# Gates of the second block as three products of split parts, with the mixers' buffers moved

## What is computed

```python
h = rmsnorm(x, norm1_g[l])
z = h @ w_in[l]
z_mla, z_nsa, z_fox, z_dsa, z_gate = split_cols(z, [MLA_COLS, NSA_COLS, FOX_COLS, DSA_COLS, GATE_COLS])
o_mla, o_nsa, o_fox, o_dsa = four attention mixers of 4 heads of 64
branches = jnp.stack([o_mla, o_nsa, o_fox, o_dsa], axis=2)
lifted = jnp.einsum('bsnc,ncd->bsnd', branches, w_branch[l])
gates = jax.nn.sigmoid(z_gate.reshape(B, S, 4, 1024))
mixed = jnp.sum(gates * lifted, axis=2)
x = x + mixed @ w_out[l]
h2 = rmsnorm(x, norm2_g[l])
x = x + jnp.square(jax.nn.relu(h2 @ w_up[l])) @ w_down[l]
```

## Time and profile before

| | us |
|---|---|
| median of three runs | 1879.98 |
| profiled execution | 1882.94 |
| its span, first to last instruction | 1881.2 |
| TensorE busy | 1702.9 (91%) |
| VectorE busy | 874.6 (46%) |
| ScalarE busy | 728.1 (39%) |
| GpSimd busy | 557.7 (30%) |
| mean granted TensorE clock | 0.950 of full |

### The profile page before, as it was taken

How to read it: one execution, slowest core, us unless ns; L and a number is a source line. 1 busy time by engine, 2 the same in 40 slices (tenths; PEclk the granted TensorE clock), 3 DMA queues, 4 the chain that set the end, 5 groups by cost and what they waited for, 6 DMA issues and landing times.

```text
span 1881.2 us, 21970 instructions
## 1 busy us (share of the span) xinstructions
PE 1702.9 (91%) x8908; PEld 1385.5 (74%) x8908; DVE 874.6 (46%) x1587; ACT 728.1 (39%) x1030; POOL 557.7 (30%) x190
## 2 busy tenths in 40 slices
PE   6999989989787799897999977999999999879997
PEld 1844767776586677777888765999888887659996
DVE  1865567765364887535233254222351432542321
ACT  2423367543232676334222343444441123444442
POOL 0400015524211155325200016564531000355554
PEclk9999789999888899998989999999999999989999
DMA  9367169955360589642342415455533433145551
GB/s 386 133 231 267 56 248 343 341 210 195 109 243 15 205 331 342 239 135 88 110 149 90 157 47 177 136 191 188 170 118 113 148 117 114 61 157 178 192 182 43
DMA packets 46645, 327.17 MB, mean 174 GB/s; under 512 B 5456, under 2 KB 5456, under 8 KB 8784
## 3 DMA queue, kind: packets, MB, share of 16 engines
q1 hardware_dynamic: 46544, 325.76, 48.5%
HBM read 324.69 MB, written 1.05 MB: 173 GB/s over the span
## 4 chain that ended last, share of the span: by engine, by line
PE 72%; DVE 18%; ACT 4%; DMA 2%; issue 1%; POOL 1%; SPq 0%; DVEq 0%; ACTq 0%; POOLq 0%
PE ps L201 27%; PE ps L204 14%; PE ps L205 14%; PE ps L206 14%; DVE lo L212 6%; DVE acc L220 2%; ACT hi L209 2%; DMA raw<-in_wmod 1%; DVE hTl L212 1%; DVE xn L212 1%; DVE gl L212 1%; PE ps L2556 1%; DMA raw<-in_wgu 1%; DVE ar L212 1%; DVE x L212 1%
## 5 line engine op out<-in xcount | busy, mean ns | idle before, releaser
L212 POOL TENSOR_TENSOR lo<-raw,hi 128x2048 fp32r<-128x2048 f32 (+2 forms) x100 | 466.3, 4674 | 717.5 <-ACT hi L209 717.5
L209 ACT ACTIVATE hi<-raw 128x2048 fp32r<-128x2048 f32 (+2 forms) x216 | 396.2, 1864 | 70.4 <-DMA raw<-in_wo_hx 28.6
L212 DVE TENSOR_TENSOR lo<-raw,hi 128x2048 fp32r<-128x2048 f32 (+1 forms) x116 | 324.5, 2814 | 125.2 <-ACT hi L209 125.2
L201 PE MATMUL ps<-hT,raw 128*128 128x256 f32 x1024 | 234.5, 386 | 0.0
L201 PEld LDWEIGHTS ps<-hT,raw 128*128 128x128 f32 x1024 | 193.7, 192 | 30.4 <-issue 3.6
L204 PE MATMUL ps<-hTh,hi 128*128 128x256 f32 x640 | 183.7, 287 | 4.6 <-POOL hTl L212 4.6
L205 PE MATMUL ps<-hTl,hi 128*128 128x256 f32 x640 | 183.0, 286 | 0.0
L206 PE MATMUL ps<-hTh,lo 128*128 128x256 f32 x640 | 182.9, 286 | 0.0
L204 PE MATMUL ps<-hi,gh 128*128 128x512 f32 x320 | 133.1, 416 | 14.4 <-DVE lo L212 14.4
L204 PE MATMUL ps<-hi,hTh 128*128 128x512 f32 (+3 forms) x320 | 118.7, 371 | 17.9 <-DVE hTl L212 10.5
L212 POOL TENSOR_TENSOR big<-big 128x512 f32<-128x512 f32 x16 | 20.3, 1269 | 376.9 <-DVE big L220 376.9
(11 more groups left out here) (285 smaller groups left out, 2836.7 us busy)
## 6 DMA issues: line engine op xcount, KB each, us to landing
raw<-in_wgu SPq DMA_DIRECT2D x64, 1024.0 KB, 5.3
raw<-in_wmod SPq DMA_DIRECT2D x48, 1024.0 KB, 5.3
raw<-in_wdn SPq DMA_DIRECT2D x32, 1024.0 KB, 4.9
raw<-in_wgt SPq DMA_DIRECT2D x32, 1024.0 KB, 4.8
raw<-in_wup SPq DMA_DIRECT2D x32, 1024.0 KB, 4.8
raw<-in_wdown SPq DMA_DIRECT2D x32, 1024.0 KB, 5.1
raw<-in_wz SPq DMA_DIRECT2D x12, 1024.0 KB, 4.8
raw<-in_wbr SPq DMA_DIRECT2D x8, 1024.0 KB, 6.9
```

The costliest lines, as they stand in the source:

```text
L201: return self.e.matmul(o, l, r, start=first, stop=last)
L209: return self.e.activation(o, a, f, **kw)
L212: return self.e.tensor_tensor(o, a, b, op)
```

## The change

The gates' chunks become split chunks ("dve"): ScalarE writes the high part, VectorE the low part over the raw chunk, and a gate is eight `mm3` with `hTh` and `hTl` in place of eight float32 matmuls with `hT`. `a_fill` and `v_fill` split gt0 and gt1 before the first gate, and after every second gate (after g1 gt2, after g3 gt3, and so on to gt15 after g27) the chunk two further. While the mixers run, the high parts have a ring of two buffers: the one left before, and the memory of `hT`, which the gates no longer read (free from the new key "z done"). The raw ring has four slots (RMIX) in place of five. The fifth holds the transposed probabilities `pT` and the compressed windows' small tiles (`up`). The probabilities `pbs` move from `ar` to the memory of `oh` and `ohT` (`pb`). The chunks of compress (cmp, two) are asked for just before their products, behind gt0 and gt1 in the queue where they were behind gt0 alone. The chunk of latent (mla) is asked for behind gt12.

```diff
-NR, RFREE, NH = 7, 5, 5
+NR, RFREE, RMIX, NH = 7, 5, 4, 5
@@ class Book
-        self.before = dict(R=[None] * NR, H=[None] * NH)
+        self.before = dict(R=[None] * NR, H=[None] * (NH + 1))
...
-    def enter(self):
+    def enter(self, free, *key):
 
         self.epoch += 1
-        self.rings["R"] = [r for r in self.rings["R"] if r < RFREE]
+        if key:
+            self.rings["H"], self.before["H"][NH] = [NH - 1, NH], key
+        self.rings["R"] = [r for r in self.rings["R"] if r < free]
 
     def leave(self, *key):
 
         self.epoch += 1
-        self.rings["R"] += range(RFREE, NR)
+        back = [r for r in range(NR) if r not in self.rings["R"]]
+        self.rings["R"] += back
         self.rings["H"] = [NH - 1, *range(NH - 1)]
-        self.before["R"][RFREE:] = [key] * (NR - RFREE)
-        self.before["H"][:-1] = [key] * (NH - 1)
+        for r in back:
+            self.before["R"][r] = key
+        self.before["H"][:NH - 1] = [key] * (NH - 1)
...
     if name == "gt":
-        return t_in["wgt"][at[0], at[1], at[2]], "raw"
+        return t_in["wgt"][at[0], at[1], at[2]], "dve"
@@ class Tiles
-        self.hi = [at(f"hi{i}", a, PIECE, dt=F32R) for i, a in enumerate(hs)]
+        self.hi = [at(f"hi{i}", a, PIECE, dt=F32R) for i, a in enumerate([*hs, self.hTat])]
...
+        self.up, self.pb = at("up", rs[RMIX], 2048), at("pb", ohat, 2048)
@@ views2
-        V.pbs = [ar[:, 4096:5120], ar[:, 5120:6144]]
+        V.pbs = [pb[:, 0:1024], pb[:, 1024:2048]]
...
-                 for p in (ar[:, 6144:7680], gr[:, 0:1536])]
-        V.cmpb = ar[:, 7680:8080]
+                 for p in (up[:, 0:1536], gr[:, 0:1536])]
+        V.cmpb = up[:, 1536:1936]
@@ t_fill
                 if n % 2 == 0:
                     c = t.chunk("gt", l, d, n // 2)
-                    wv = kn(c.raw, 8)
+                    wh, wl = kn(c.hi, 8), kn(c.lo, 8)
                 b = t.take("B", "gate", l, d, n)
-                t.wait_ge(*t.at("landed", c.key))
+                t.wait_ge(*t.at("lo", c.key))
                 t.wait_ge(*t.free(b))
                 for k in range(8):
-                    m = t.mm(self.ps[:, b, 0:256], wv[:, k, 128 * (n % 2):128 * (n % 2) + 128], self.hT[:, k, :],
-                             k == 0, k == 7)
+                    m = t.mm3(self.ps[:, b, 0:256], [q[:, k, 128 * (n % 2):128 * (n % 2) + 128] for q in (wh, wl)],
+                              [q[:, k, :] for q in self.H3], k == 0, k == 7)
@@ a_fill
         a.wait_ge(*a.at("used", ("z", l, 5, 1)))
+        self.a_split(a, "gt", l, 0, 0, ahead=1)
         for d in range(8):
             for n in range(4):
...
                 a.ac(V.sg[:, n, d, :], self.ps[:, b, 0:256], ACT.Tanh, scale=0.5).then_inc(*a.up(f"free{b}"))
+                if n % 2:
+                    self.a_split(a, "gt", l, d, n // 2, ahead=2)
                 yield
@@ v_fill
+        self.v_split(v, "gt", l, 0, 0, ahead=1)
         for d in range(8):
             for n in range(4):
+                if n % 2:
+                    self.v_split(v, "gt", l, d, n // 2, ahead=2)
                 yield
@@ t_compress
-        w2 = [t.chunk("cmp", l, s) for s in range(2)]
...
         for s in range(2):
-            wcv = w2[s].raw.rearrange("p (m d) -> p m d", m=32)
-            t.wait_ge(*t.at("landed", w2[s].key))
+            c = t.chunk("cmp", l, s)
+            wcv = c.raw.rearrange("p (m d) -> p m d", m=32)
+            t.wait_ge(*t.at("landed", c.key))
@@ t_latent
-        wm = t.chunk("mla", l)
         yield
...
         yield
+        wm = t.chunk("mla", l)
         t.wait_ge(*t.at("landed", wm.key))
@@ tensor, first block
-        t.book.enter()
+        t.book.enter(RFREE)
@@ tensor, second block
             self.t_z(t, l)
-            t.book.enter()
+            t.mark("z done", l)
+            t.book.enter(RMIX, "z done", l)
             self.t_mixers(t, l)
```

More of the change, by code:

```diff
@@ L368, in __init__ @@
         self.z = sb("z", 2, 2520)
+        ohat = self.where
         self.oh, self.ohT = sb("oh", 2, 640, dt=F32R), sb("ohT", 5, 256, dt=F32R)
@@ L1988, in views2 @@
     def views2(self):
-        ar, big = self.ar, self.big
+        ar, up, pb, big = self.ar, self.up, self.pb, self.big
         A = lambda a, n, i: ar[:, a:a + n].rearrange("p (i n) -> p i n", i=i)
@@ L2389, in t_compress @@
             m.then_inc(*t.up(f"full{b}" if s else "pe"))
-            t.mark("used", w2[s].key)
+            t.mark("used", c.key)
         yield
```

## The result

The changed kernel takes 1903.19 us (median of four, 1902.27 to 1906.17) beside 1879.98: the ratio is 1.012, with a 95% interval of 1.0095 to 1.0144. The forecast had the sign right (slower) and less than half of the size: +9.5 us against +23. The profiled execution took 1902.27 us with a span of 1900.5, where that of before had 1882.94 and 1881.2.

A forecast was written before the change was run, and what follows sets the result against it. TensorE was taken as the bound, with almost no idle time in the gates. Per layer, 21.4 us of waits less 17.6 saved, plus 1.2 for the clock, gave +10 us over two layers: 1889.5 us, range 1864 to 1905.

The forecast's parts named there:

- The saving: Gates on TensorE: 2.88 us each in place of 3.43, saving 17.6 us a layer if nothing waits.
- The moves at no cost: Moved buffers and chunks cost nothing; if the cover for the last chunks is gone, up to 3 us a layer.
- Place 1: Start of the gates: 4.9 us idle before g0, then 2.1 behind index rotations and key copies; together 7.0.
- Place 2: Compressed windows: chunk gt2 lands late and its high part delays the window copies; 2.5 us idle.
- Place 3: Compressed probabilities: VectorE reaches them late, between low parts 6 and 7; 1.0 us, an estimate of 0 to 2.
- Place 4: First softmaxes: low parts among top-k passes, then exps and chunk 10's split delay g20; 2.7 us idle.
- Place 5: Latent: 1.5 us idle behind nwin maxima and latent norms, then 2.8 before g22; together 4.3.
- Place 6: Banks: 2.1 us idle inside the latent transposes and 1.8 before g28; together 3.9.
- The clock: TensorE's granted clock falls once a layer after idle time: +1.2 us a layer, 0 to 4 possible.
- the fall at every wait: Rival: the clock falls at all six places, 1.5 us each; +3.8 + 9 a layer, 1905 us, chance 0.12.
- the cover holds: Rival: only places 1 and 2 stay, 9.5 of 17.6 us; -8 a layer, 1864 us, chance 0.24.
- Half of them: Rival: places 3 to 6 cost 7 to 9 us in place of 11.9; within 3.8 us of 1880, chance 0.16.

The follow-up runs named there:

- the products alone: Changed kernel with three float32r products a step but nothing split, normed rows' parts as weights: 1849.55 us, ratio 0.983 to the kernel before.
- the moves alone: Changed kernel's buffers, ring and chunk order, with gates back to raw float32 products and nothing split: 1880.66 us, ratio 0.9999 to the kernel before.
- the waits filled: Changed kernel plus unused float32r matmuls before g0, the compressed windows, g20 and g22: 1894.23 us, ratio 1.0071 to the kernel before.

## Why the prediction was right in sign and wrong in size

- **The saving** (17.6 us a layer): right. 18.5 and 17.0 measured with the products alone. By its own row it should have been higher: 16 starts 0.217 apart are 3.47 us a gate and not 3.43, so 0.59 saved and 18.9 a layer.
- **The moves at no cost**: right, ratio 0.9999. The sign that I had given for the contrary, lifts of over 69 us, did come (70.7), but it was a poor sign: with the moves alone they are 69.7 us, at a clock of 0.95 as here, in a kernel that isn't slower.
- **The places of the waits** (21.4 us a layer): right in kind and nearly in size, 18.5. Place 1: 4.9 forecast, 4.7 measured; its second wait of 2.1 didn't come. The index rotations took 2.1 us where I took 2.7, and g0 at the low clock took 4.4 and covered the rest; with g0 at full clock 0.7 of it is there (the waits filled). Place 2: 2.5 forecast, 4.6 measured. TensorE's work behind g1 took 7.6 us as forecast (7.5); the difference is that GpSimd's copies for the windows took 4.6 us (938.7 to 943.3) where I took the 2.5 of before. The first of them ran beside low part 2 on VectorE. Place 3: 1.0 and 0.7. Place 4: 2.7 and 2.4. Place 5: 4.3 and 2.9. Place 6: 3.9 and 3.2. Taken together, waits less saving are 0.0 in layer 0 and +1.5 us in layer 1 where I had +3.8.
- **The clock** (+1.2 us a layer): this is the step that failed. It was 9.4 us in layer 0 and 10.7 in layer 1. I took one fall a layer from the stretch behind 1090 us, and named the fall at every wait as a rival of 0.12 with +9 a layer. That rival's size was right, in part by luck: it had 1.5 us at each of six places, and the runs show no fall at some and more than that at others.
- **What the clock cost, by gates.** Counted against the products alone, layer 0 pays 1.3 us at g0 (4.2 for 2.9), 3.3 at the small matmuls (13.8 for 10.5), 1.4 at g20 and g21 (7.3 for 5.9) and 2.6 at g28 and g29 (8.4 for 5.8), less 0.2 at g4. Sum 8.4. The other 1.0 of the 9.4 is in the steps just ahead of the waits, by up to 0.16 us at each of the eight: the record of the last matmul is 0.28 us long, where the next one would have started after 0.12 (an estimate; the heads' transposes ahead of g0, 0.97 us for 0.82, show it). Layer 1 pays 1.6 at g0, 1.8 at the small matmuls, 1.7 at g20 and g21, 2.4 at g22, 1.5 at g28 and g29, and 1.7 in smaller pieces. What I missed most in layer 0 are the small matmuls. I treated them as a cover, 10.35 us long whatever happened, and they are themselves what TensorE's clock stretches; the row of before already had a mean clock of 0.71 for them. Their length also varies by 1 us and more with no wait ahead, so that the shares of single pieces are no better known than that.
- The Trainium skill (TensorE: Matmul & The Clock Gate, HAM oscillation — how this bites in real kernels) has a kernel in which waits between groups make each group start cold. It tells this of waits of some 3 to 5 us for a DMA, so my reading that by it a loss would come at every one of the six places went further than the Trainium skill does. In the runs the clock fell at the two places with waits of that length (4.7 and 4.6 us), in both layers. It also fell behind shorter ones: at g20 (2.4) and g28 (1.5 and 1.7) in both layers, at g22 (2.7) in layer 1 alone, and not behind the 0.7. That is four of six places in layer 0 and five in layer 1, with about 31 and 41 us at half clock in the two stretches where before had 10. The row that I preferred, a clock of 0.98 in the lifts, has waits behind other mixes of work and wasn't the nearest case.
- **The rivals**: that the cover holds (0.24) is out. It needed places 3 to 6 to overlap, and each is in the list of waits. *Half of them* (0.16) nearly had its waits: places 3 to 6 measured 9.2 us where it took 7 to 9. Its time, within 3.8 us of 1880, didn't come, because the clock came on top. That float32r runs no faster is out by the products alone.
- What would show it right was there: released by `DVE lo` before g0, g20, g22; ScalarE waiting for a DMA of gates once; stretches longer than 148.5. They were 158 and 161 in place of 152 to 154, and the clock (0.90, 0.87) was under the 0.93 that I had given as the sign that the falls decide.

Not tried: a third buffer for the high parts, which would let a chunk be split before the gates two chunks back are done. I don't know of free memory for it. Why the clock falls behind the 2.7 us before g22 in one layer and not in the other stays open. That fall alone is 2.4 of layer 1's 10.7 us. With the waits filled, the stretches are 154.3 and 154.2.

## What to carry to other kernels

When a step on a full TensorE is made shorter by giving other engines work, ask where in their fixed orders that work stands, not whether they have room in total: by the stretches, 63 us of splits a layer on engines that were idle for 98 and 110 of 148.5 us (VectorE and ScalarE) cost 18.5 us of waits, and most of the loss went with the moving of four of them. Price each new wait with the slow matmuls behind it too: here they cost half as much again as the waits themselves (9.4 and 10.7 us on 18.5). A wait that can't be moved can be made cheaper by filling it, but only if nothing else is due right behind.

## What the runs showed of the hardware

- Idle time of 2.4 to 4.7 us on TensorE, and two waits of 1.5 and 1.7 us close together, were followed by matmuls at 1.2 GHz (g28 and g29 8.5 us for 6.0). Not always: behind the same 2.7 us the granted clock was 1.00 in layer 0 and 0.50 in layer 1. With unneeded matmuls in four of these waits, the gates and small matmuls behind them ran as before: adding 14 us of work a layer (115 matmuls of 0.12) took 9 us off the kernel.
- The 128 small matmuls (64 x 64 weights, 16 columns) leave no idle time on TensorE, and the granted clock falls during them all the same: mean 0.71 before, with no wait ahead.
- An instruction of VectorE on 128 x 4 elements takes 4.2 to 4.5 us while GpSimd makes a low part (128 x 2048), and 0.17 without. The Trainium skill (GPSIMD Engine Reference, Specifications) says that the two share their interfaces to SBUF and that it is instructions with two inputs there, or in a two-port mode, that contend. The step `z<-z,rt` (4.69 us for 0.43) has two inputs and agrees. The two on four columns have one; whether they ran in such a mode the trace doesn't say. They ended about when the two low parts beside them did (1006.2 and 1010.7). A pair of small ones, as the first low part began, took 0.2 us.
